# Two-layer diffusion backbone: the MLP's second product in seven block products a pair of tiles instead of eight

## The chip, the cores and the metric

The kernel runs on one core of one Trainium2 chip. The metric is the device time of one execution in microseconds. The core has TensorE (matmul, "PE"; its loads of the stationary operand are "PEld"), VectorE ("DVE"), ScalarE ("ACT"), GpSimd ("POOL") and the queue of SyncE ("SP"), which issues transfers. Matmuls write into PSUM, eight banks of 128x512 float32 values; everything else lies in SBUF, 128 partitions wide.

## What is computed

Two layers over 1024 latent and 256 context tokens, width 1024, all in float32. Each layer mixes the tokens (long convolution, retention, attention), projects, and adds an MLP with a hidden width of 4096. The change is in the MLP alone:

```python
def squared_relu_mlp(h, w1, w2):
    return jnp.square(jax.nn.relu(h @ w1)) @ w2

x = x + ga1 * (jnp.concatenate([hy, ret, att], axis=-1) @ p['w_out'])
x = x + ga2 * squared_relu_mlp(modulate(x, p['norm2_g'], sh2, sc2), p['mlp_w1'], p['mlp_w2'])
if not last:
    xc = xc + cga2 * squared_relu_mlp(modulate(xc, p['norm2_g'], csh2, csc2), p['mlp_w1'], p['mlp_w2'])
```

Layer 0 runs the MLP over 10 tiles of 128 tokens (8 latent, 2 context), layer 1 over the 8 latent ones.

## The kernel before, in words

`build` (L3146) calls one phase after the other; `phase_out` (the output projection) comes ahead of `phase_mlp`, and in layer 0 the norm of layer 1 follows, in layer 1 `phase_final`. Each phase is a block in which every engine has its own list of instructions, joined by semaphores; a `Signal` counts on through the program, and `count` works out the value to wait for. The order on each engine is written out by hand.

A float32 product is made of three passes (`three_pass`, L150 to L154) over operands split in a high part, rounded by ScalarE (a Copy into float32r), and a low part, the rest, by a subtraction on VectorE or GpSimd: high by high, high by low, low by high.

`phase_mlp` goes through the hidden width in NB = 16 blocks of FB = 256 columns, two halves of FT = 2. The tokens lie in GROUPS of 4, 4 and 2 tiles (two groups in layer 1). In a block:

- SyncE loads the next block's w1 columns (two transfers, L2977) and w2 rows (two, L2980) into `w1_raw` and `w2_raw` as soon as the low parts of this block's have been made. The first block's loads are issued by `mlp_first_loads` (L2910, L2912) at the end of `phase_out`.
- TensorE runs `steps`: up product of group 0, up of group 1, down of group 0, up of group 2 (layer 0), down of groups 1 and 2. An up product of a half is 8 k-steps (KT) of three matmuls of up to 512 tokens into one of PSUM banks 0 to 3. A down product is made for each tile t and half h of the output, two halves f of the hidden block by three passes, 128x512, into one of banks 4 to 7.
- ScalarE takes each up product through Relu (L3000), Square (L3004) and the high part (L3008), and makes the high parts of w1 (L2991) and w2 (L2996).
- VectorE makes the low parts of w1 (L3022), w2 (L3028) and the hidden values (L3036), and multiplies each down product by the gate into `mlp_tmp` (L3044).
- GpSimd adds `mlp_tmp` to x (L3063).

x stays in SBUF throughout. When a tile of x is complete, ScalarE sums its squares for the next norm (`square_sum`, L164).

Of the kernel before, what the change touches and what calls it, by code (L numbers as in the profile page):

```python
# [19 lines left out]
F32 = mybir.dt.float32  # L20
# [5 lines left out]
P = 128  # L26
# [2615 lines left out]
def phase_out(kit, l):  # L2642
# [261 lines left out]

def mlp_first_loads(kit, l, sp):

    raw1, raw2 = kit.at("w1_raw", [P, 2, 4, FB], 152), kit.at("w2_raw", [P, FB // P, D], 160)
    w1_dram, w2_dram = kit.io["mlp_w1"][l].rearrange("(t p) n -> p t n", p=P), kit.io["mlp_w2"][l]
    for i in range(2):
        sp.dma_start(raw1[:, i], w1_dram[:, 4 * i:4 * i + 4, 0:FB]).then_inc(kit.sig(f"mlp_raw{i}", 16).sem, 16)  # L2910
    for f in range(FB // P):
        sp.dma_start(raw2[:, f], w2_dram[f * P:(f + 1) * P, :]).then_inc(kit.sig(f"mlp_raw{2 + f}", 16).sem, 16)  # L2912


def mlp_gate_loads(kit, l, sp):

    gate = kit.at("gate2", [P, 2, D], 196)
    for cond in range(2):
        sp.dma_start(gate[:, cond, :], kit.gate_dram[l, 1, cond].partition_broadcast(P)).then_inc(kit.sig("mlp_gate_in", 16).sem, 16)


def phase_mlp(kit, l):

# [9 lines left out]
    w2h, w2l = hl(kit, "w2", [P, FT, D], 136)  # L2933
    raw1, raw2 = kit.at("w1_raw", [P, 2, 4, FB], 152), kit.at("w2_raw", [P, FT, D], 160)
    hh, hlo = hl(kit, "hidden", [P, 2, FT, 512], 168)
    relu, square, tmp = (kit.at(n, [P, 2, 512], 184 + 4 * i) for i, n in enumerate(("relu", "square", "mlp_tmp")))
    gate = kit.at("gate2", [P, 2, D], 196)
    steps = [("up", 0), ("up", 1), ("down", 0)] + ([("up", 2)] if n_groups == 3 else []) + [("down", g) for g in range(1, n_groups)]
# [9 lines left out]
    w1_hi, w1_lo, w2_hi, w2_lo, up, relued, squared, h_hi, h_lo, down, gated, added = sems = [kit.sig(n) for n in names]
    growth = [2, 2, FT, FT, NU, NU, NU, NU, NU, ND, ND, ND]

    raised = (relued, h_lo, added, gated, up, down)
    for s in raised:
        s.total += 1
# [4 lines left out]
    g_in.plan(range(2))  # L2958

# [5 lines left out]

    with nc.Block() as block:
        @block.sync
        def _(sp):
            w1_dram = io["mlp_w1"][l].rearrange("(t p) n -> p t n", p=P)
            w2_dram = io["mlp_w2"][l]  # L2970


            with sp.Fori(1, NB) as b:
# [4 lines left out]
                for f in range(FT):  # L2978
                    sp.wait_ge(w2_lo.sem, count(w2_lo, b - 1, f + 1))
                    sp.dma_start(raw2[:, f], w2_dram[bass.ds(col + f * P, P), :]).then_inc(w_raw[2 + f].sem, 16)  # L2980

        @block.scalar
        def _(act):
            act.sem_inc(relued.sem, 1)
            with act.Fori(0, NB // UNROLL) as loop:
                for b in [(loop, v) for v in range(UNROLL)]:
                    for i in range(2):
                        act.wait_ge(w_raw[i].sem, count(w_raw[i], b, 16))
                        if i == 0:
                            act.wait_ge(up.sem, count(up, b, 0))  # L2990
# [303 lines left out]
```

## Time and profile before

| what | value |
|---|---|
| median of three runs | 3913.89 us (3913.44 to 3917.47) |
| the profiled execution, its own time | 3917.63 us |
| its span from first to last instruction | 3915.8 us |
| granted TensorE clock, mean over the span | 0.952 |
| instructions | 53160 |

The engine times of the page are sums of the instructions' durations. Matmuls overlap one another in such a sum, so their starts, in order of time, tell what one costs. A line of the page often is that of a helper: all matmuls of a three-pass product stand under L152, L153 and L154, whichever phase issued them, and are told apart by the names of their tiles. In order of time, a row that ends in "x2" holds two instructions that followed one another directly. The two levels of TensorE's clock, 1.2 and 2.4 GHz, stand as 0.5 and 1.0; a stretch with both shows a value between.

### The profile page before, as it was taken

To read this page: it belongs to the slowest core of one execution; us is meant where nothing else is said; L and a number is where in the kernel's file an instruction comes from. 1 tells how busy PE (TensorE), PEld (TensorE's weight loads), DVE (VectorE), ACT (ScalarE), POOL (GpSimd) and SP (SyncE) were. 2 spreads that over 40 slices of the span, in tenths; PEclk is the share of its full clock that TensorE was granted. 3 is DMA by queue.
4 is the path that set the end of the run, shared out by engine and by line. 5 is a ranking of instruction groups with operands and counts; after the bars stand their busy time and mean duration, and the time that the engine had idled before them with its cause. 6 is when DMAs were issued, how large, how long until landed. Compare 5 with 4: busy or idle time off the path is not lost. (4 is left out here: it accounts for less than half of the span.)

```text
span 3915.8 us, 53160 instructions
## 1 busy us (share of the span) xinstructions
PE 3633.8 (93%) x19584; PEld 3052.4 (78%) x19584; DVE 2121.0 (54%) x3713; ACT 1412.3 (36%) x2831; POOL 1400.5 (36%) x1268
## 2 busy tenths in 40 slices
PE   7979998999679899999999899989997989999997
PEld 3668997777667688888888679978886768888886
DVE  5468535666676444444444574356675645444544
ACT  3341124666513522222222411246672252222222
POOL 1122133555100055444554421436630005445554
PEclk8989987999889999999999899879998999999999
DMA  5255201001313111111101162010014311111111
GB/s 208 93 174 183 94 10 35 12 8 40 150 63 152 44 44 32 32 43 43 43 28 37 70 200 83 11 32 11 6 39 167 151 44 54 54 43 43 54 54 48
DMA packets 153895, 266.96 MB, mean 68 GB/s; under 512 B 8968, under 2 KB 122777, under 8 KB 151290
## 3 DMA queue, kind: packets, MB, share of 16 engines
q1 hardware_dynamic: 143452, 212.38, 16.3%
q0 software_dynamic: 6352, 46.01, 3.1%
q10 hardware_dynamic: 3920, 6.29, 0.5%
q8 instruction: 107, 1.75, 0.2%
q14 instruction: 64, 0.52, 0.0%
HBM read 229.10 MB, written 33.59 MB: 67 GB/s over the span
## 5 line engine op out<-in xcount | busy, mean ns | idle before, releaser
L3063 POOL TENSOR_TENSOR x<-x,mlp_tmp 128x512 f32<-128x512 f32 x576 | 785.6, 1397 | 1324.0 <-DVE mlp_tmp L3044 1319.2
L3044 DVE TENSOR_TENSOR mlp_tmp<-psum,gate 128x512 f32<-128x512 f32 x576 | 391.8, 689 | 273.1 <-POOL x L3063 194.6
L152 PE MATMUL psum<-act_hi,w_hi 128*128 128x512 f32 (+1 forms) x1280 | 472.5, 369 | 14.1 <-DVE w_lo L3022 14.1
L153 PE MATMUL psum<-act_lo,w_hi 128*128 128x512 f32 (+1 forms) x1280 | 472.2, 369 | 0.0
L154 PE MATMUL psum<-act_hi,w_lo 128*128 128x512 f32 (+1 forms) x1280 | 471.9, 369 | 0.0
L152 PE MATMUL psum<-w_hi,hidden_hi 128*128 128x512 f32 x1152 | 449.9, 391 | 0.0
L153 PE MATMUL psum<-w_lo,hidden_hi 128*128 128x512 f32 x1152 | 448.4, 389 | 0.0
L154 PE MATMUL psum<-w_hi,hidden_lo 128*128 128x512 f32 x1152 | 448.2, 389 | 0.0
L3036 DVE TENSOR_TENSOR hidden_lo<-square,hidden_hi 128x512 fp32r<-128x512 f32 x160 | 102.3, 640 | 591.8 <-ACT hidden_hi L3008 591.8
L1981 DVE TENSOR_REDUCE att_max<-psum 128x1 f32<-128x512 f32 (+2 forms) x272 | 217.3, 799 | 261.9 <-PE psum L154 261.8
L3000 ACT ACTIVATE relu<-psum 128x512 f32<-128x512 f32 x160 | 88.9, 555 | 665.9 <-PE psum L154 665.9
L152 PEld LDWEIGHTS psum<-act_hi,w_hi 128*128 128x128 f32 x1280 | 242.2, 189 | 55.5 <-DVE w_lo L3022 14.9
L153 PEld LDWEIGHTS psum<-act_lo,w_hi 128*128 128x128 f32 x1280 | 242.2, 189 | 40.8
L154 PEld LDWEIGHTS psum<-act_hi,w_lo 128*128 128x128 f32 x1280 | 242.2, 189 | 40.2
L1805 ACT ACTIVATE probs<-psum,att_max 128x512 f32<-128x512 f32 (+2 forms) x272 | 208.7, 772 | 176.6 <-DVE att_max L1985 175.9
L152 PE MATMUL psum<-w_in_hi,act_hi 128*128 128x256 f32 (+1 forms) x912 | 259.1, 284 | 0.0
L154 PE MATMUL psum<-w_in_hi,act_lo 128*128 128x256 f32 (+1 forms) x912 | 256.7, 282 | 0.0
L153 PE MATMUL psum<-w_in_lo,act_hi 128*128 128x256 f32 (+1 forms) x912 | 256.7, 281 | 0.0
L152 PEld LDWEIGHTS psum<-w_hi,hidden_hi 128*128 128x128 f32 x1152 | 216.3, 188 | 47.5 <-DVE mlp_tmp L3044 3.7
L154 PEld LDWEIGHTS psum<-w_hi,hidden_lo 128*128 128x128 f32 x1152 | 216.3, 188 | 45.2
L153 PEld LDWEIGHTS psum<-w_lo,hidden_hi 128*128 128x128 f32 x1152 | 216.4, 188 | 43.9
L2996 ACT ACTIVATE w_hi<-w_raw 128x1024 fp32r<-128x1024 f32 x64 | 64.3, 1052 | 467.1 <-PE psum L154 467.1
(385 smaller groups left out, 8242.4 us busy)
## 6 DMA issues: line engine op xcount, KB each, us to landing
w_raw<-in_mlp_w SPq DMA_DIRECT2D x128, 512.0 KB, 3.8
side_w<-in_w_ada SPq DMA_DIRECT2D x40, 1024.0 KB, 6.3
w_raw<-in_w_in SPq DMA_DIRECT2D x32, 512.0 KB, 4.8
hy_ahead<-in_hy_ahead POOLq DMA_DIRECT2D x8, 2048.0 KB, 12.5
open_tab<-in_hy_ahead POOLq DMA_DIRECT2D x8, 1024.0 KB, 13.5
spec_scratch<-open_staged SPq DMA_DIRECT2D x16, 512.0 KB, 2.7
hy_spec<-spec_scratch SPq DMA_DIRECT2D x16, 512.0 KB, 3.6
hy_back<-in_hy_back POOLq DMA_DIRECT2D x2, 4096.0 KB, 29.7
```

The lines of the kernel that those rows point to most:

```text
L152: pe.matmul(out, lhs[0], rhs[0], start=start, stop=False)
L153: pe.matmul(out, lhs[0], rhs[1], start=False, stop=False)
L154: return pe.matmul(out, lhs[1], rhs[0], start=False, stop=stop)
L1805: act.activation(pe_[:, n % 2, at:end], psf[:, at:end], ACT.Exp, scale=SCALE, bias=mx[:, n % 2, 1:2], accum_out=sums[:, k, n % SUM_RING:n ...
L1981: dve_last = dve.tensor_reduce(mx[:, n % 2, 6 + k:7 + k], psf[:, at:at + len(part) * P], AX.X, ALU.max)
L2996: act.activation(w2h[:, f], raw2[:, f], ACT.Copy).then_inc(w2_hi.sem, 1)
L3000: act.activation(relu[:, i % 2, 0:n], ps[:, i % 4, 0:n], ACT.Relu).then_inc(relued.sem, 1)
L3036: dve.tensor_tensor(hlo[:, g % 2, f, 0:n], square[:, i % 2, 0:n], hh[:, g % 2, f, 0:n].bitcast(F32), ALU.subtract).then_inc(h_lo.sem, 1)
L3044: dve.tensor_tensor(tmp[:, j % 2, :], ps[:, 4 + j % 4, :], gate[:, int(t >= LAT_TILES), 512 * h:512 * h + 512], ALU.mult).then_inc(gated.s ...
L3063: pool.tensor_tensor(a, a, tmp[:, j % 2, :], ALU.add).then_inc(added.sem, 1)
```

## The change

The hidden block (256 tokens of a pair of tiles by 256 hidden columns) and the block of w2 (256 rows by 1024 columns) are each taken as two by two blocks. The product of two such is made of seven block products of sums of the blocks, where there were eight of the blocks themselves. `STEPS` names for each of the seven the slot of hidden sums and the slot of weight sums.

- **TensorE**: `product` makes one block product of three 128x128 by 128x512 matmuls into one bank of 4 to 7; there are 7 a pair (35 a block in layer 0, 28 in layer 1). The up product of group 0 of the next block is made during the last down group: from its fourth k-step on, each k-step is followed by one (layer 0) or two (layer 1) block products until they are all issued.
- **Weights**: SyncE loads w2's rows straight into slots 0 to 3 of `w2_sums`, and waits for all products of the block before. VectorE makes three more slots (and overwrites one) in four dependent subtractions, 128x512 each; ScalarE makes the high parts of slots 0 to 2 and 3 to 6, VectorE the low parts, in the place of the sums.
- **Hidden values**: ScalarE squares straight into slots of `hid_sums`; VectorE makes four dependent sums of 128x128 a pair; then one high part (ScalarE) and one low part (VectorE) of 128x896.
- **Adding up**: ScalarE copies the first product of a pair out of PSUM; VectorE makes seven additions out of PSUM (`add_up`), into x or into two scratch tiles; GpSimd makes four additions of scratch tiles to x (`add_shared`).
- **w1's low parts** are made by GpSimd, but for the first block's.
- **Gate and residual**: `phase_out` stores x to a scratch tensor in DRAM and no longer loads the gate. In the MLP x is set to zero by VectorE and collects the bare product. At the end SyncE loads the gate and the old x (once the last up product has been made), and `gated_tile` makes x * gate + old x, two instructions of 128x1024 a tile, on GpSimd for tiles 0 to 2 and on VectorE for the others. The squares for the norm come behind.
- Some semaphores are given back between phases (`kit.retire`).

The core of the diff:

```diff
@@ phase_out, SyncE
-            sp.wait_ge(c_lo.sem, c_lo[(3, 1)])
-            mlp_gate_loads(kit, l, sp)
-            sp.wait_ge(done.sem, done[units[-1]])
-            mlp_first_loads(kit, l, sp)
+            for j, t in enumerate(range(0, n_tiles, 4)):
+                n = min(4, n_tiles - t)
+                if t + n == n_tiles:
+                    sp.wait_ge(done.sem, done[units[-1]])
+                    mlp_first_loads(kit, l, sp)
+                sp.wait_ge(added.sem, added[(t + n - 1, 1)])
+                sp.dma_start(kit.x_dram[t * P:(t + n) * P].rearrange("(t p) n -> p t n", p=P), x[:, t:t + n, :]).then_inc(x_kept.sem, 16)
@@ phase_mlp
+STEPS = [(0, 0), (5, 1), (3, 4), (4, 2), (1, 5), (2, 3), (6, 6)]
...
+    def gated_tile(eng, sem, t):
+        c = int(t >= LAT_TILES)
+        eng.tensor_tensor(x[:, t, :], x[:, t, :], gate[:, c, :], ALU.mult).then_inc(sem.sem, 1)
+        eng.wait_ge(sem.sem, sem[(t, 0)])
+        eng.wait_ge(x_in[t // 4].sem, x_in[t // 4][0])
+        eng.tensor_tensor(x[:, t, :], x[:, t, :], x_old[:, t, :], ALU.add).then_inc(sem.sem, 1)
@@ SyncE
             with sp.Fori(1, NB) as b:
                 col = sp.snap(b * FB)
...
-                for f in range(FT):
-                    sp.wait_ge(w2_lo.sem, count(w2_lo, b - 1, f + 1))
-                    sp.dma_start(raw2[:, f], w2_dram[bass.ds(col + f * P, P), :]).then_inc(w_raw[2 + f].sem, 16)
+                sp.wait_ge(down.sem, count(down, b, 0))
+                mlp_w2_rows(kit, l, sp, col)
+            sp.wait_ge(up.sem, count(up, NB, 0))
+            for cond in range(2):
+                sp.dma_start(gate[:, cond, :], kit.gate_dram[l, 1, cond].partition_broadcast(P)).then_inc(g_in.sem, 16)
+            sp.wait_ge(x_kept.sem, kept)
+            for j, t in enumerate(range(0, n_tiles, 4)):
+                n = min(4, n_tiles - t)
+                sp.dma_start(x_old[:, t:t + n, :], kit.x_dram[t * P:(t + n) * P].rearrange("(t p) n -> p t n", p=P)).then_inc(x_in[j].sem, 16)
@@ ScalarE
+            def square(b, p):
+                act.wait_ge(relued.sem, count(relued, b, 2 * (p // 2) + 2))
+                act.wait_ge(down.sem, count(down, b, M * (p - 1)))
+                cols = slice(p % 2 * 2 * P, (p % 2 + 1) * 2 * P)
+                for f in range(FT):
+                    act.activation(hs[buffer(b, p)][:, 5 * f:5 * f + 2].rearrange("p a c -> p (a c)"), relu[f][:, cols],
+                                   ACT.Square).then_inc(squared.sem, 1)
+            def high(b, p):
+                act.wait_ge(h_sum.sem, count(h_sum, b, 4 * p + 4))
+                act.activation(hh[buffer(b, p)][:], hs[buffer(b, p)][:], ACT.Copy).then_inc(h_hi.sem, 1)
+            def copy(b, p):
+                act.wait_ge(down.sem, count(down, b, M * p + 1))
+                act.wait_ge(added.sem, count(added, b, 4 * (p - 1)))
+                act.activation(p1[buffer(b, p)][:], ps[:, 4 + M * p % 4, :], ACT.Copy).then_inc(copied.sem, 1)
+            def one_block(b, following):
...
+                copy(b, 0)
+                if n_groups == 2 and following is not None:
+                    w1_high(following)
+                copy(b, 1)
+                for p in (2, 3):
+                    square(b, p)
+                    high(b, p)
+                if n_groups == 3:
+                    positive(b, 2, 0)
+                    positive(b, 2, 1)
+                copy(b, 2)
+                if n_groups == 3 and following is not None:
+                    w1_high(following)
+                copy(b, 3)
+                if n_groups == 3:
+                    square(b, 4)
+                    high(b, 4)
+                    copy(b, 4)
@@ VectorE
+            dve.wait_ge(x_kept.sem, kept)
+            dve.memset(x[:, 0:n_tiles, :], 0.0).then_inc(zeroed.sem, 1)
...
+            def hidden_sums(b, p):
+                s = hs[buffer(b, p)]
+                dve.wait_ge(squared.sem, count(squared, b, 2 * p + 2))
+                for k, (to, i, j, op) in enumerate(((2, 1, 6, ALU.add), (1, 0, 1, ALU.subtract), (3, 2, 0, ALU.subtract),
+                                                    (4, 5, 3, ALU.subtract))):
+                    if k:
+                        dve.wait_ge(h_sum.sem, count(h_sum, b, 4 * p + k))
+                    dve.tensor_tensor(s[:, to], s[:, i], s[:, j], op).then_inc(h_sum.sem, 1)
+            def add_up(b, p, between=None):
...
+                dve.wait_ge(added.sem, count(added, b, 4 * (p - 1)))
+                for k, (out, other, n, own) in enumerate(...):
+                    dve.wait_ge(down.sem, count(down, b, M * p + n + 1))
...
+                    dve.tensor_tensor(out, other, ps[:, 4 + (M * p + n) % 4, :], ALU.add).then_inc(summed.sem, 1)
+                    if k == 3 and between is not None:
+                        hidden_sums(b, between)
...
+                    weight_sums(b)
+                    weight_low(b, 0)
+                    hidden_sums(b, 0)
+                    hidden_sums(b, 1)
+                    weight_low(b, 1)
+                    hidden_low(b, 0)
+                    hidden_low(b, 1)
+                    add_up(b, 0)
+                    add_up(b, 1, 2)
+                    hidden_low(b, 2)
+                    hidden_sums(b, 3)
+                    hidden_low(b, 3)
+                    add_up(b, 2)
+                    if NP == 4:
+                        add_up(b, 3)
+                    else:
+                        add_up(b, 3, 4)
+                        hidden_low(b, 4)
+                        add_up(b, 4)
@@ GpSimd
+            def add_shared(b, p):
+                i = buffer(b, p)
+                for what, half, h, behind in ((p1[i], 0, 0, 1), (u2[i], 0, 1, 5), (u3[i], 1, 1, 6), (u3[i], 1, 0, 7)):
+                    a = x[:, 2 * p + half, 512 * h:512 * h + 512]
...
+                    pool.wait_ge(summed.sem, count(summed, b, M * p + behind))
+                    pool.tensor_tensor(a, a, what[:], ALU.add).then_inc(added.sem, 1)
+            def one_block(b, following):
+                w1_at = 0 if n_groups == 2 else 2
+                for p in pairs:
+                    if p == w1_at and following is not None:
+                        w1_low(following)
+                    add_shared(b, p)
@@ TensorE
+            def product(b, j):
+                p, n = divmod(j, M)
...
+                if n == 0:
+                    if p == 0:
+                        pe.wait_ge(w2_lo.sem, count(w2_lo, b, 2))
+                    pe.wait_ge(h_lo.sem, count(h_lo, b, p + 1))
+                i, (u, w) = buffer(b, p), STEPS[n]
+                three_pass(pe, ps[:, 4 + j % 4, :], [a[i][:, u, :] for a in (hh, hlo)],
+                           [a[:, w, :] for a in (w2h, w2l)], True, True).then_inc(down.sem, 1)
+            def one_block(b, following):
+                for g in groups[1:]:
+                    up_group(b, g)
+                    down_group(b, g - 1)
+                if following is None:
+                    down_group(b, n_groups - 1)
+                else:
+                    j, each = 2 * M * (n_groups - 1), GROUPS[n_groups - 1][1] // 2
+                    for f in range(FT):
+                        for k in range(KT):
+                            up_step(following, 0, f, k)
+                            if f * KT + k >= 3:
+                                for _ in range(min(each, ND - j)):
+                                    product(b, j)
+                                    j += 1
```

## Rows read from the trace of the kernel before

**Rows 1.** The page: busy time, share of the span and instructions.
```profile
PE 3633.8 (93%) x19584; PEld 3052.4 (78%) x19584; DVE 2121.0 (54%) x3713; ACT 1412.3 (36%) x2831; POOL 1400.5 (36%) x1268
```

**Rows 2.** Table of stretches; columns: start:end, us, busy PE, PEld, DVE, ACT, POOL, PEclk, DMA, GB/s.
```profile
1341.40:2219.20 877.80, 877.76 (x4224) 742.10 (x4224) 381.81 (x478) 228.17 (x367) 432.24 (x319) 1.00 0.12 36
2219.20:2222.90 3.70, 0.15 (x1) 0.00 (x0) 0.69 (x1) 1.86 (x4) 2.14 (x2) 0.93 0.00 0
3194.95:3894.90 699.95, 699.94 (x3072) 576.69 (x3072) 331.42 (x382) 186.68 (x267) 349.05 (x255) 1.00 0.15 45
3894.90:3898.50 3.60, 0.17 (x1) 0.00 (x0) 0.69 (x1) 1.89 (x4) 2.16 (x2) 0.98 0.00 0
```

**Rows 3.** Order of time, TensorE in an up product; columns: start us, us, engine, line.
```profile
1358.99 0.39 PE L152 MATMUL psum<-act_hi,w_hi 128*128 128x512 f32 x1
1359.22 0.39 PE L153 MATMUL psum<-act_lo,w_hi 128*128 128x512 f32 x1
1359.44 0.39 PE L154 MATMUL psum<-act_hi,w_lo 128*128 128x512 f32 x1
```

**Rows 4.** Groups by line: one of the second product's three matmul groups.
```profile
L152 PE MATMUL psum<-w_hi,hidden_hi 128*128 128x512 f32 x1152 | 449.9, 391 | 0.0
```

**Rows 5.** Single lines (ns min/median/max), one row by time, one group by line (mean).
```profile
L3044 DVE TENSOR_TENSOR mlp_tmp<-psum,gate x576: 670/691/694, 1367.9 to 3895.1; 128x512 f32<-128x512 f32 x192
...
1422.62 1.28 DVE L3044 TENSOR_TENSOR mlp_tmp<-psum,gate 128x512 f32<-128x512 f32 x2
...
L3063 POOL TENSOR_TENSOR x<-x,mlp_tmp x576: 1260/1296/2297, 1368.7 to 3895.9; 128x512 f32<-128x512 f32 x192
...
L3022 DVE TENSOR_TENSOR w_lo<-w_raw,w_hi x64: 1214/1628/2315, 1340.2 to 3842.9; 128x1024 fp32r<-128x1024 f32 x64
...
L1571 DVE TENSOR_TENSOR k_rope_tmp<-mla,rope 128x128 f32<-128x128 f32 x2 | 0.6, 283 | 0.0
...
L1233 POOL TENSOR_TENSOR w_in_lo<-w_raw,w_in_hi x32: 1569/2400/2678, 247.2 to 2450.4; 128x1024 fp32r<-128x1024 f32 x28, 128x640 fp32r<-128x640 f32 x4
...
L752 DVE TENSOR_TENSOR factor<-factor,side_gain x6: 167/168/2355, 462.8 to 2398.8; 128x8 f32<-128x8 f32 x6
```

**Rows 6.** Order of time: VectorE and GpSimd, both reading SBUF, 1448 to 1452.
```profile
1448.20 3.45 DVE L3022 TENSOR_TENSOR w_lo<-w_raw,w_hi 128x1024 fp32r<-128x1024 f32 x2
1448.36 2.20 POOL L3063 TENSOR_TENSOR x<-x,mlp_tmp 128x512 f32<-128x512 f32 x1
...
1449.33 2.31 DVE L3022 TENSOR_TENSOR w_lo<-w_raw,w_hi 128x1024 fp32r<-128x1024 f32 x1
```

**Rows 7.** The first weight loads, lines L2910 (first pair) and L2912 (second).
```profile
L2910 SPq DMA_DIRECT2D w_raw<-in_mlp_w x4: 384/446/509, 1324.6 to 3178.6; - x4
...
DMA to landing us min/median/max: 3.8/4.3/4.9
...
DMA to landing us min/median/max: 5.5/6.2/6.8
```

**Rows 8.** Groups by line, ScalarE, 1400 to 2190: the high parts.
```profile
L2996 ACT ACTIVATE w_hi<-w_raw 128x1024 fp32r<-128x1024 f32 x29 | 29.2, 1052 | 183.1 <-PE psum L154 183.1
```

**Rows 9.** Table of stretches: TensorE after a wait (columns as in rows 2).
```profile
2959.00:2963.90 4.90, 0.01 (x1) 0.02 (x1) 4.73 (x6) 0.60 (x1) 0.00 (x0) 0.85 1.04 421
2963.90:2970.00 6.10, 6.09 (x29) 6.10 (x30) 0.00 (x0) 0.00 (x0) 0.00 (x0) 0.51 1.04 426
```

**Rows 10.** Groups by line: a memset; the page's DMA issues (KB each, us to landing).
```profile
L1456 DVE MEMSET ret_state<- 64x256 f32 x2 | 0.5, 272 | 0.0
...
gate<-gate_scratch SPq DMA_DIRECT2D x8, 512.0 KB, 11.7
x<-x_scratch SPq DMA_DIRECT2D x2, 2048.0 KB, 18.9
```

More of the change, by code:

```diff
@@ L2932, in phase_mlp @@
     w1h, w1l = hl(kit, "w1", [P, KT, FB], 120)
[L2933 to L2938, printed above, removed]
@@ L2948, in phase_mlp @@
[L2948 to L2951 removed]
+    w2h, w2l, w2s = kit.at("w2x_hi", [P, 7, 512], 136, F32R), kit.at("w2x_lo", [P, 7, 512], 160, F32R), kit.at("w2_sums", [P, 7, 512], 160)
+    raw1 = kit.at("w1_raw", [P, 2, 4, FB], 152)
+    hs = [kit.at("hid_sums", [P, 7, P], 174 + 3.5 * i) for i in range(2)]
@@ new lines, in phase_mlp @@
+    pairs = range(n_tiles // 2)
+    NP, M = len(pairs), len(STEPS)
+    NU, ND = len(ups), NP * M
+    w_raw = [kit.sig(f"mlp_raw{i}", 16) for i in range(4)]
+    g_in, norm_squared, x_kept, zeroed = kit.sig("mlp_gate_in", 16), kit.sig("nt_squared"), kit.sig("mlp_x_out", 16), kit.sig("nt_meaned")
+    x_in = [kit.sig(f"out_x{j}", 16) for j in range(3)]
+    by_pool, by_dve = kit.sig("out_gated"), kit.sig("out_added")
+    pool_tiles, dve_tiles = range(0, 3), range(3, n_tiles)
+    square_order = [3, 4, 0, 5, 6, 1, 7] + list(range(8, n_tiles)) + [2]
@@ L2958, in phase_mlp @@
     g_in.plan(range(2))
+    for sg in x_in:
+        sg.plan(range(1))
+    by_pool.plan([(t, k) for t in pool_tiles for k in range(2)])
+    by_dve.plan([(t, k) for t in dve_tiles for k in range(2)])
     def count(s, b, k):
@@ L3049, in _ @@
+            w1_high(0)
+            with act.Fori(0, NB // UNROLL - 1) as loop:
                 for v in range(UNROLL):
@@ L3055, in _ @@
         @block.gpsimd
         def _(pool):
-            pool.sem_inc(added.sem, 1)
-            with pool.Fori(0, NB // UNROLL) as loop:
-                for b in [(loop, v) for v in range(UNROLL)]:
-                    for j, (g, t, h) in enumerate(downs):
-                        a = x[:, t, 512 * h:512 * h + 512]
-                        pool.wait_ge(gated.sem, count(gated, b, j + 1))
-                        pool.tensor_tensor(a, a, tmp[:, j % 2, :], ALU.add).then_inc(added.sem, 1)
+            pool.sem_inc(added.sem, 8)
@@ new lines, in one_block @@
+            def one_block(b, following):
[4 more added lines that the diff above has]
+                    add_shared(b, p)
+            with pool.Fori(0, NB // UNROLL - 1) as loop:
+                for v in range(UNROLL):
+                    one_block((loop, v), (loop, v + 1))
+            for b in range(NB - UNROLL, NB):
+                one_block(b, b + 1 if b + 1 < NB else None)
@@ L3100, in phase_final @@
+            up_group(0, 0)
+            with pe.Fori(0, NB // UNROLL - 1) as loop:
+                for v in range(UNROLL):
+                    one_block((loop, v), (loop, v + 1))
+            for b in range(NB - UNROLL, NB):
+                one_block(b, b + 1 if b + 1 < NB else None)
 def phase_final(kit):
```

249 lines of the change are left out of this document (144 added, 105 removed).

## The prediction

> **What bounds the kernel now.** I read the busy table first: TensorE is busy for 93% of the span, VectorE 54%, GpSimd 36% [rows 1]. Then a table of stretches: the two MLPs take 877.8 and 699.95 us, and in both TensorE's busy time is the whole stretch, at the full granted clock, 2.4 GHz [rows 2]. Sixteen blocks each: 54.9 and 43.7 us a block. After the last matmul 3.7 and 3.6 us pass before the next phase. In order of time, consecutive 128x512 matmuls start 0.227 us apart [rows 3]. So until now only the count of matmuls sets the MLP, and everything else hides in it.
>
> **What is removed.** A pair of token tiles needed 8 block products, now 7, each three matmuls: 0.68 us. There are five pairs in layer 0, four in layer 1, so 15 and 12 matmuls fewer a block, 432 in all, from three groups of 1152 [rows 4]: 432 x 0.227 = 97.9 us. Ideal blocks are then 51.5 and 41.0 us. This holds only if the new sums stay beside it.
>
> **What is added, and at what price.** A 128x512 addition out of PSUM is priced by today's product of PSUM and gate: 670 to 694 ns in all 576 cases, although GpSimd was at work beside many of them; two take 1.28 [rows 5]. Seven a pair are 4.5 us against 4.8 us of products: just hidden. A subtraction of 1024 elements from SBUF takes 1.22 us at its shortest, so 1536, 2048 and 896 elements (hidden low) about 1.76, 2.29 and 1.09; one of 128 takes 0.283 [rows 5]. The 20 hidden sums and 5 low parts of a layer 0 block, with the weight sums, bring VectorE to about 42 us of the 51. GpSimd keeps 20 additions of 1.30 and gains two 1024-wide ones of 2.4. Neither is full. What matters is order: VectorE works through a hand-written list.
>
> **The lock.** The longest durations show what happens when both engines read SBUF. A GpSimd addition starts at 1448.36, in the middle of a VectorE subtraction, and takes 2.20 instead of 1.30; the next subtraction, started at 1449.33, takes 2.31 instead of 1.22 and ends 1.08 after GpSimd does [rows 6]. They take turns, a whole instruction each. A tiny one pays as well: 128x8 elements, 168 ns in the median, took 2355 ns once, about one 1024-wide GpSimd instruction [rows 5]. So each of four dependent hidden sums can wait for one GpSimd addition: 4 x (1.14 + 0.16) = 5.2 us, less what the first finds already done, for 1.2 us alone. The row is for 128x8; no row has a 128x128 sum under GpSimd additions. By the Trainium skill, "SBUF — State Buffer", section "SBUF: two separate sides", the shared port pair is locked for a whole instruction and the loser blocks fully; that speaks against this change, and rows 6 agree.
>
> **Step 1, the turn to new weights.** w2's rows now load only when the last product of the block before is done, at T. TensorE then has six k-steps of the next up product and the 10.9 us of group 1 left: 15.0 us. Against it: the two loads are issued by T+0.9, and the first pair of four such loads landed in 3.8 to 4.9 us [rows 7], so T+5.6. Then VectorE: four sums 2.8, low part 1.76, two times four hidden sums 2.4, low part 2.29, hidden low 1.09: 10.3 us. The first product starts at T+16.0: a stall of 1.0. Bounds: 0 (landing in 3.8) and 2.9 (6.8, the second pair [rows 7]). By the Trainium skill, "VectorE: DVE Perf Modes", the section on the TRN2 errata, an SBUF instruction takes 58 cycles plus one per element; that makes this chain about 8.7 us and the stall nothing. The rows of 0.283 and 1.22 us contradict it.
>
> **Step 2, inside the block.** Times from the first product. Layer 1: products of pairs 0 and 1 end at 9.5, four k-steps at 12.3. GpSimd has w1's low parts until 7.4, then additions without a gap. VectorE's fourth addition of pair 1 ends at 9.1; the hidden sums of pair 2 take turns until 13.9, three additions until 15.7, hidden low until 16.8. So product 14 waits 4.6 us. Hidden sums and low of pair 3, with ScalarE's high part (0.95, from 1.05 per 1024 elements [rows 8]) between, then hold VectorE and the copy of pair 2's first product until 22: 1.1 more. Stall 5.7. Layer 0: the third up group (5.9 us) hides pair 2, and 1.7 is left from pair 3; but the sums of pair 4 meet GpSimd straight behind w1's low parts, from 26.1 to 30.8, and its hidden low ends at 34.3 where TensorE is ready at 29.3: 5.1. Stall 6.8. Without turns the same count gives 1.1 and 1.0; these are the low bounds. If the waiting instruction is late, its queue too is late: all additions of the next pair stand behind it.
>
> **Step 3, the clock.** After 4.9 us in which TensorE did nothing (busy 0.01), it worked 6.1 us at 0.51, thus 1.2 GHz [rows 9]. Waits of 4.6 and 5.1 us in each block should do the same. Five us at half speed lose 2.5; I take 2.0 in layer 0, where products follow at once, and 1.0 in layer 1, where a second wait hides some. Bounds 0 and 3.
>
> **Step 4, the ends.** Before the first block VectorE clears x: 272 ns for 256 elements [rows 10], so 10.9 us for 10240; with the 10.3 us chain it ends just ahead of the 23.8 us that TensorE spends on two up groups: nothing. If the cover went, it would cost up to 11, once a layer. The store of x and its reload (2 MB in 18.9 us, gate 11.7 [rows 10]) lie beside 20 us of products; the reload would be the next thing late. Behind the last product the additions end at +3.4. Then gate and residual: 14 instructions of 1024 on VectorE (layer 0; 10 in layer 1), 6 on GpSimd. In turns: six rounds of 1.12 + 2.35 = 20.8 us, then eight of 1.2 (four): 30.4 (25.6). With the squares 36.6 and 31.7, against 3.7 and 3.6: +33 and +28. If both ran side by side it would be +18 and +16, the low bounds.
>
> **The sum.** Layer 0: 51.5 + 1.0 + 6.8 + 2.0 = 61.3 for 54.9, +6.4; layer 1: 41.0 + 1.0 + 5.7 + 1.0 = 48.7 for 43.7, +5.0. Over 15 blocks 96 + 75. The last blocks, without a turn, add 5 each. Ends 61. In all +242 on the profiled execution (3917.6 by its own clock, span 3915.8), 3.7 above the median of 3913.9: about 4156.
>
> **Rivals.** *The lock hardly bites small sums.* For it: 128 elements need the port for a tenth of a microsecond, and no row has just this pair of instructions. Against it: the 2355 ns. Then stalls are 1.0 + 1.0 and 1.0 + 1.1, the clock stays, blocks 53.5 and 43.1: 16 blocks give -22 and -10, ends +34 to +61: about 3918 to 3950. Half bitten, up to 4050. *Faster: the sums are truly hidden.* The place is the hidden sums behind pair 1: if GpSimd has its additions done before VectorE comes to them, and the weight rows land by T+4.6, no wait is left and only the ends cost: -98 + 34 = -64, 3850. It decides below 1.15 us of stall a block (98 less 61, over 32). For it: GpSimd's list is only 31 us of a block. Against it: this list lies just there, directly behind the products. *The clock pays more.* It falls in both waits and slows the products that release VectorE: 2 to 3 us more a block, 4220 to 4250. That the change does something else than it says has no hold in the diff: 7 products of three matmuls stand there.
>
> **Chances.** Forecast, 4050 to 4220: 0.56. Lock light, 3918 to 4050: 0.2. Faster: 0.13. Clock: 0.11. The range takes in the first two and half of the clock's case: 3925 to 4235; the faster case and a rest stay out. A measurement of this kernel tells 0.2% (8 us) from no change; only the lower edge of the light lock is within: 0.05. Faster 0.13, slower 0.82.
>
> **What would show it.** Right: the MLPs' stretches near 979 and 780 us, TensorE idle ahead of the product matmuls until VectorE's hidden low, 128x128 sums with a median far above 0.283 and many above 1.2 us, a granted clock below 1 in the MLPs, 30 us or so between the last matmul and the next phase. Wrong: hidden sums of 0.3 us, a clock of 1.00, stretches below 860 and 690, or TensorE waiting for the weights' DMA rather than for VectorE.

## The result, and the profile after

| what | before | after |
|---|---|---|
| median | 3915.5 us (3913.44 to 3917.47, 4 runs) | 4167.14 us (4149.13 to 4175.33, 4 runs) |
| the profiled execution, span | 3915.8 us | 4173.5 us |
| granted TensorE clock, mean | 0.952 | 0.924 |
| layer 0 MLP, first to last matmul; then to the next phase | 877.9; 3.6 us | 986.4; 35.7 us |
| layer 1 MLP, the same | 700.1; 3.6 us | 788.7; 31.6 us |

Slower by a ratio of 1.0636, 95% interval 1.060 to 1.0673. The forecast was 4156, the range 3925 to 4235. The four differences of the table, 108.5 + 32.1 + 88.6 + 28.0 = 257.2 us, are all but 0.5 of the 257.7 by which the span grew; the stretches outside the MLPs and their ends differ by 1.1 us at most. (The last two lines come from the order of time, as do the same lines in the table further down.)

The page's first part and three of its groups by line (busy us, mean ns | idle before, releaser), to be held against [rows 1, 4]:

```profile
PE 3633.4 (87%) x19152; PEld 3014.9 (72%) x19152; DVE 2837.4 (68%) x4799; ACT 1565.8 (38%) x3087; POOL 1570.8 (38%) x1340
...
L152 PE MATMUL psum<-w2x_hi,hid_hi 128*128 128x512 f32 x1008 | 423.4, 420 | 199.2 <-DVE hid_lo L3152 178.4
...
L3147 DVE TENSOR_TENSOR hid_sums<-hid_sums 128x128 f32<-128x128 f32 x576 | 347.6, 608 | 14.8
...
L3060 ACT ACTIVATE hid_hi<-hid_sums 128x896 fp32r<-128x896 f32 x144 | 137.2, 954 | 460.7 <-DVE hid_sums L3147 460.7
```

432 matmuls fewer, and TensorE's busy time is the same. One of the three product groups was idle 199 us before its matmuls where the group of before had 0.0 [rows 4], nearly all until VectorE's hidden low part. That waits for ScalarE's high part, which waits for the hidden sums: 608 ns in the mean each. The table of stretches (columns as in [rows 2]):

```profile
1342.30:2329.20 986.90, 878.35 (x3984) 717.57 (x3984) 745.97 (x1058) 297.84 (x478) 501.33 (x348) 0.94 0.11 38
2329.20:2364.60 35.40, 0.00 (x0) 0.00 (x0) 30.07 (x16) 11.17 (x20) 23.09 (x9) 0.56 0.00 0
3336.50:4127.60 791.10, 697.51 (x2880) 563.62 (x2880) 627.52 (x866) 254.13 (x382) 407.93 (x285) 0.95 0.14 47
4127.60:4156.20 28.60, 0.00 (x0) 0.00 (x0) 24.39 (x10) 8.63 (x15) 21.57 (x8) 0.52 0.00 0
```

Of 986.90 us TensorE works 878.35, and the granted clock is 0.94 where it was 1.00. VectorE, at 76% of the stretch, is not full, nor is GpSimd. So it looks like order and not load; the experiments put that to the test. One block of layer 0 in order of time, on VectorE, GpSimd, ScalarE and TensorE in turn (a row that ends in x4 is four instructions in a row):

```profile
1764.01 4.35 DVE L3147 TENSOR_TENSOR hid_sums<-hid_sums 128x128 f32<-128x128 f32 x4
1768.28 1.87 DVE L3167 TENSOR_TENSOR x<-x,psum 128x512 f32<-128x512 f32 x3
1770.08 1.59 DVE L3152 TENSOR_TENSOR hid_lo<-hid_sums,hid_hi 128x896 fp32r<-128x896 f32 x1
...
1764.30 3.91 POOL L3216 TENSOR_TENSOR x<-x,mlp_u 128x512 f32<-128x512 f32 x3
...
1768.39 0.95 ACT L3060 ACTIVATE hid_hi<-hid_sums 128x896 fp32r<-128x896 f32 x1 [6.76 <-DVE hid_sums L3147]
...
1771.72 0.80 PE L152 MATMUL psum<-w2x_hi,hid_hi 128*128 128x512 f32 x1 [4.27 <-DVE hid_lo L3152]
1772.31 0.63 PE L153 MATMUL psum<-w2x_lo,hid_hi 128*128 128x512 f32 x1
```

Read from the bottom. TensorE stood for 4.27 us and then ran with starts 0.43 us apart where [rows 3] have 0.227: 1.2 GHz, the lower of its two levels. It waited for a hidden low that ended at 1771.67, behind three additions, behind four sums that took 4.35 us. Exactly beside these GpSimd made three additions of 1.3 without a pause. Four sums with three additions between them: they take turns. The same place in layer 1 shows the sums of pairs 2 and 3 one behind the other, and the first of the two waits of the forecast:

```profile
3565.29 4.82 DVE L3147 TENSOR_TENSOR hid_sums<-hid_sums 128x128 f32<-128x128 f32 x4
3570.03 1.87 DVE L3167 TENSOR_TENSOR x<-x,psum 128x512 f32<-128x512 f32 x3
3571.82 1.18 DVE L3152 TENSOR_TENSOR hid_lo<-hid_sums,hid_hi 128x896 fp32r<-128x896 f32 x1
3572.93 3.29 DVE L3147 TENSOR_TENSOR hid_sums<-hid_sums 128x128 f32<-128x128 f32 x4
...
3573.05 0.80 PE L152 MATMUL psum<-w2x_hi,hid_hi 128*128 128x512 f32 x1 [4.42 <-DVE hid_lo L3152]
```

The turn to new weights, on SyncE's queue, VectorE and TensorE. After the last product TensorE goes on at 1783.04; VectorE starts on the weights at 1789.23, TensorE on the first product at 1799.60, late by 1.44.

```profile
1783.37 0.57 SPq L2925 DMA_DIRECT2D w_sums<-in_mlp_w  x1
1784.14 0.44 SPq L2926 DMA_DIRECT2D w_sums<-in_mlp_w  x1
...
1789.23 2.87 DVE L3132 TENSOR_TENSOR w_sums<-w_sums 128x512 f32<-128x512 f32 x4 [5.31 <-DMA w_sums<-in_mlp_w]
...
1798.46 2.09 DVE L3152 TENSOR_TENSOR hid_lo<-hid_sums,hid_hi 128x896 fp32r<-128x896 f32 x2
...
1799.60 0.50 PE L152 MATMUL psum<-w2x_hi,hid_hi 128*128 128x512 f32 x1 [1.44 <-DVE hid_lo L3152]
```

And the end of layer 0, gate and residual: while GpSimd has tiles left, each instruction of either engine takes 3.2 to 3.4 us; alone VectorE takes 1.23.

```profile
2337.20 3.36 DVE L3006 TENSOR_TENSOR x<-x,gate 128x1024 f32<-128x1024 f32 x1
...
2336.28 3.20 POOL L3009 TENSOR_TENSOR x<-x,x_old 128x1024 f32<-128x1024 f32 x1
...
2353.72 1.23 DVE L3009 TENSOR_TENSOR x<-x,x_old 128x1024 f32<-128x1024 f32 x1
```

### The profile page after: what moved, and what is told of

Read it like the earlier page. It is cut to its first block and busy times, and to the rows that moved or that the text cites. A ratio compares the mean times of both kernels' runs of the same rounds, so it can differ in the third digit from the quotient of the medians.

```text
span 4173.5 us, 55995 instructions
## 1 busy us (share of the span) xinstructions
PE 3633.4 (87%) x19152; PEld 3014.9 (72%) x19152; DVE 2837.4 (68%) x4799; ACT 1565.8 (38%) x3087; POOL 1570.8 (38%) x1340
## 5 line engine op out<-in xcount | busy, mean ns | idle before, releaser
L3216 POOL TENSOR_TENSOR x<-x,mlp_u 128x512 f32<-128x512 f32 x432 | 590.3, 1395 | 199.7 <-DVE x L3167 199.7
L152 PE MATMUL psum<-w2x_hi,hid_hi 128*128 128x512 f32 x1008 | 423.4, 420 | 199.2 <-DVE hid_lo L3152 178.4
L3167 DVE TENSOR_TENSOR x<-x,psum 128x512 f32<-128x512 f32 x720 | 468.3, 683 | 160.4 <-PE psum L154 149.8
L3216 POOL TENSOR_TENSOR x<-x,mlp_p 128x512 f32<-128x512 f32 x144 | 187.2, 1300 | 667.9 <-DVE x L3167 667.9
L153 PE MATMUL psum<-w2x_lo,hid_hi 128*128 128x512 f32 x1008 | 411.4, 408 | 0.0
L154 PE MATMUL psum<-w2x_hi,hid_lo 128*128 128x512 f32 x1008 | 410.4, 407 | 0.0
L152 PEld LDWEIGHTS psum<-w2x_hi,hid_hi 128*128 128x128 f32 x1008 | 200.1, 199 | 280.3 <-DVE hid_lo L3152 144.0
L3147 DVE TENSOR_TENSOR hid_sums<-hid_sums 128x128 f32<-128x128 f32 x576 | 347.6, 608 | 14.8
L3205 POOL TENSOR_TENSOR w_lo<-w_raw,w_hi 128x1024 fp32r<-128x1024 f32 x60 | 143.4, 2411 | 526.9 <-ACT w_hi L3041 526.9
L154 PEld LDWEIGHTS psum<-w2x_hi,hid_lo 128*128 128x128 f32 x1008 | 200.2, 199 | 45.2
```

What stands on the lines that cost most here:

```text
L152: pe.matmul(out, lhs[0], rhs[0], start=start, stop=False)
L153: pe.matmul(out, lhs[0], rhs[1], start=False, stop=False)
L154: return pe.matmul(out, lhs[1], rhs[0], start=False, stop=stop)
L3147: dve.tensor_tensor(s[:, to], s[:, i], s[:, j], op).then_inc(h_sum.sem, 1)
L3167: dve.tensor_tensor(out, other, ps[:, 4 + (M * p + n) % 4, :], ALU.add).then_inc(summed.sem, 1)
L3205: pool.tensor_tensor(w1l[:, 4 * i:4 * i + 4, :], raw1[:, i], w1h[:, 4 * i:4 * i + 4, :].bitcast(F32), ALU.subtract).then_inc(w1_lo.sem, 1)
```

## The experiments

The ratio is to executions of the kernel before that were made together with the variant's (their medians lie between 3914.1 and 3918.6 us). MLP is first to last matmul, end is from there to the next phase's first instruction, both from the profiled executions, layer 0 / layer 1. The profiled execution of the change, 4175.3 us, was the slowest of its four, so differences of traces come out up to 8 us larger than those of medians.

| kernel | median us (runs) | ratio to before (95%) | MLP | end |
|---|---|---|---|---|
| the change | 4167.1 (4) | 1.0636 (1.060 to 1.0673) | 986.4 / 788.7 | 35.7 / 31.6 |
| shared additions cut short | 3956.2 (2) | 1.0106 (1.0086 to 1.0127) | 863.8 / 703.3 | 33.4 / 28.7 |
| ends on VectorE | 4153.5 (4) | 1.0606 (1.0589 to 1.0624) | 986.0 / 786.0 | 29.4 / 25.2 |
| sums on GpSimd | 4020.3 (4) | 1.0269 (1.0251 to 1.0286) | 888.4 / 735.2 | 38.7 / 33.0 |
| wait filled | 4127.5 (4) | 1.0550 (1.0532 to 1.0567) | 954.9 / 773.0 | 35.7 / 31.5 |
| products denser | 4123.3 (4) | 1.0535 (1.0517 to 1.0553) | 958.3 / 768.0 | 35.7 / 31.6 |
| new orders | 3908.4 (11) | 0.9984 (0.9974 to 0.9993) | 842.2 / 681.1 | 31.0 / 25.0 |
| new orders, new ends | 3893.7 (6) | 0.9942 (0.9930 to 0.9954) | 841.9 / 675.6 | 26.2 / 21.6 |
| and the ends' turns | 3895.1 (5) | 0.9946 (0.9933 to 0.9960) | 841.7 / 677.5 | 23.9 / 19.8 |

**Shared additions cut short.** Is it the turns with GpSimd?

```diff
-                    pool.tensor_tensor(a, a, what[:], ALU.add).then_inc(added.sem, 1)
+                    pool.tensor_tensor(a[:, 0:8], a[:, 0:8], what[:, 0:8], ALU.add).then_inc(added.sem, 1)
```

> GpSimd's shared additions (add_shared) touch 8 of their 512 columns; the other 504 are left out, nothing else differs, and every wait stays. If the turns that the hidden sums take with these additions are the cause, a block's period falls from 61.6 to about 53.3 us in layer 0 and from 49.1 to about 43 us in layer 1 (the wait for new weights of 1.4 us stays), TensorE's waits of 4.3 and 4.4 us for the hidden low part shrink to about 1, the granted clock in both MLPs is 1.00, and the whole is near 3950 us. If VectorE's own load and the order of its list are the cause, the additions are innocent: periods stay within 1 us of 61.6 and 49.1 and the whole above 4130 us.

3956.2: 211 us less, near the 3950 that the turns were to give. The tile's own durations (ns, minimum/median/maximum), first of the change, then of this variant:

```profile
L3147 DVE TENSOR_TENSOR hid_sums<-hid_sums x576: 282/293/1383, 1359.2 to 4115.4; 128x128 f32<-128x128 f32 x192
```

```profile
L3147 DVE TENSOR_TENSOR hid_sums<-hid_sums x576: 281/292/295, 1353.6 to 3895.4; 128x128 f32<-128x128 f32 x192
```

The sums themselves were not touched, and not one of 576 is above 295 ns now. The MLPs lose 122.6 and 85.4 us, and the granted clock is back at 1.00:

```profile
1336.90:2201.00 864.10, 832.46 (x3984) 694.49 (x3984) 646.44 (x1057) 301.38 (x478) 157.80 (x348) 1.00 0.13 44
```

What is left above the ideal 16 x 51.5 = 824 are, by the gaps between starts, a wait of some 1.4 us a block at the turn to new weights, which this edit leaves alone, and one of 0.9 for the high part of pair 4. The edit also takes work off GpSimd (158 us in this stretch for 501), so by itself it does not tell the turns from GpSimd's load; the variant with the sums on GpSimd does. Note the median of the first line, 293: most sums are made while GpSimd is idle. The slow minority lies where it decides, and a median hides that.

**Ends on VectorE.** All tiles' gate and residual on VectorE, none on GpSimd, the squares in the order of the tiles.

```diff
-    pool_tiles, dve_tiles = range(0, 3), range(3, n_tiles)
+    pool_tiles, dve_tiles = range(0), range(n_tiles)
```

> Gate and residual of all tiles on VectorE, none on GpSimd. If the two engines take whole turns when both read SBUF, GpSimd's six instructions cost 2.1 us of turn each where VectorE's cost 1.15: the stretch behind the last product gets shorter although one engine does it all, from 29.4 to 24 us in layer 0 and from 24.6 to 19 us in layer 1, 10 to 11 us in all (about 4156 us). If they share, or run side by side, taking GpSimd's help away lengthens it: 14 instructions become 20 (layer 0) and 10 become 16 (layer 1), 7 us more each, about 4180 us.

4153.5, 13.6 less, with intervals that overlap; what shows it is the trace, where the ends are 6.3 and 6.4 us shorter and the MLPs the same within 3. In turns, this helper costs more than it takes over.

**Sums on GpSimd.** If GpSimd makes the hidden sums of pairs 2 and up itself, between its additions, there is nobody to take turns with.

```diff
 VectorE, in add_up, behind the fourth addition
-                        hidden_sums(b, between)
+                        hidden_low(b, between)
 VectorE, its list
-                    add_up(b, 1, 2)
+                    add_up(b, 1)
                     hidden_low(b, 2)
-                    hidden_sums(b, 3)
-                    hidden_low(b, 3)
-                    add_up(b, 2)
+                    add_up(b, 2, 3)
...
 GpSimd, layer 1 (in layer 0: shared 0, sums 2 and 3, shared 1, w1's low parts, sums 4, shared 2 to 4)
+                    w1_low(following)
+                    hidden_sums(b, 2)
+                    add_shared(b, 0)
+                    hidden_sums(b, 3)
+                    add_shared(b, 1)
```

> The hidden sums of pairs 2, 3 and 4 are made by GpSimd, between its own additions, so that they never have to take turns with them; VectorE's low part of pair 3 (and 4) stands behind the fourth addition of the pair before. The number of instructions is the same. If the turns are the cause, TensorE's waits inside a block nearly go, the clock stays at 1.00, periods fall to 53 to 54 us in layer 0 and 42.5 to 43.5 us in layer 1, and the whole to 3940 to 3970 us. If the order of VectorE's list alone mattered, half of that; if the load on the engines is the cause, nothing goes, as GpSimd gets even more to do: above 4130 us.

4020.3: 147 us less, but 50 above the upper edge of what was expected. The MLPs lose 98.0 and 53.5 us although GpSimd does more than in the change (584 us of layer 0's MLP for 501), so it was not its load. The sums take no turns any more and the clock is 1.00 in layer 0 and 0.99 in layer 1; a turn is left where VectorE's hidden low meets GpSimd, up to 1.93 us for 1.09. Four sums take GpSimd 2.07 us (GpSimd, ScalarE and VectorE in layer 1):

```profile
3550.19 2.07 POOL L3222 TENSOR_TENSOR hid_sums<-hid_sums 128x128 f32<-128x128 f32 x4
...
3552.29 0.95 ACT L3060 ACTIVATE hid_hi<-hid_sums 128x896 fp32r<-128x896 f32 x1 [6.33 <-POOL hid_sums L3222]
3553.15 0.58 ACT L3065 ACTIVATE mlp_p<-psum 128x512 f32<-128x512 f32 x1
...
3553.83 0.69 DVE L3167 TENSOR_TENSOR mlp_u<-mlp_p,psum 128x512 f32<-128x512 f32 x1 [2.79 <-ACT mlp_p L3065]
```

What I had not counted is the next wait behind the one removed. ScalarE sits 6.33 us in front of the high part of pair 3, and the copy of pair 2's first product, ready long before, stands behind it; VectorE waits 2.79 us for that copy, and TensorE up to 1.5 us for the PSUM bank that it frees. Both queues are in the wrong order for a wait that now ends later.

**Wait filled.** What does the lower clock cost by itself? TensorE makes 18 matmuls that nobody reads (into bank 3, free then) ahead of the product that waits longest.

```diff
+                    if fill and p == 2 * (n_groups - 1):
+                        for _ in range(6):
+                            three_pass(pe, ps[:, 3, :], [a[:, 0, 0:P] for a in (w1h, w1l)], [a[:, 0, 0:512] for a in (xh, xl)], True, True)
```

> Ahead of the product that waits for 4.3 us (layer 0) and 4.4 us (layer 1), TensorE makes 18 matmuls of 128x512 that nobody reads, 4.1 us at full speed, into a free bank of PSUM; the wait itself stays. If the clock is granted at half speed because of this wait, it stays at 1.00 now, and periods fall by 2.5 to 3 us in layer 0 and by 1.2 to 2.3 us in layer 1 (there a second wait, of 1.1 us, comes out that the slow clock hides): 55 to 80 us in all, 4090 to 4110 us. If the clock costs nothing, since VectorE is what products wait for anyway, the time stays within 10 us of 4167; if the matmuls outlast the wait, it is longer.

4127.5, 39.6 less, against 57 to 77 for the expected 4090 to 4110. The clock's part is there: the first product behind the wait is at full speed at once,

```profile
1753.30 0.50 PE L152 MATMUL psum<-w2x_hi,hid_hi 128*128 128x512 f32 x1 [0.26 <-DVE hid_lo L3152]
1753.64 0.40 PE L153 MATMUL psum<-w2x_lo,hid_hi 128*128 128x512 f32 x1
```

and the MLPs get 31.5 and 15.7 us shorter. Fifteen of the sixteen blocks have the fill, so that is 2.1 and 1.05 a block. It is what full clock gives back, and smaller than I had expected here: VectorE's work is as late as before, and faster matmuls only reach the next wait sooner. In layer 1 two such waits, which the change does not have, come out in each block; by the starts they are 0.5 and 0.4 us (the brackets count from a matmul's modelled end):

```profile
3347.00 0.50 PE L152 MATMUL psum<-w2x_hi,hid_hi 128*128 128x512 f32 x1 [0.35 <-ACT mlp_p L3065]
...
3348.24 0.50 PE L152 MATMUL psum<-w2x_hi,hid_hi 128*128 128x512 f32 x1 [0.28 <-DVE x L3167]
```

**Products denser.** Is the turn to new weights a matter of cover? The last pairs' products end earlier.

```diff
-                    j, each = 2 * M * (n_groups - 1), GROUPS[n_groups - 1][1] // 2
+                    j, each = 2 * M * (n_groups - 1), GROUPS[n_groups - 1][1] // 2 + 1
```

> The products of the last pairs follow one another closer between the steps of the next first product (two a step for one in layer 0, three for two in layer 1), so that the last of them ends 2 us (3 steps of 0.68) and 1.4 us (2 steps) earlier and the new second weights have that much more cover. Nothing is left out. The theory that the wait at the turn (1.44 us in layer 0, 1.38 in layer 1) is what the chain of new weights is late by: it goes, about 1.4 us a block in both layers, 32 blocks, some 4120 us in all, with the waits before products 14 and 28 as they are. Rival, VectorE has no time to give there: the products wait for VectorE's additions of the pair before (a wait for a PSUM bank inside the stretch takes the place of the one at the turn), and the time stays within 10 us of 4167.

4123.3, 43.8 less, where some 4120 was expected; the MLPs 28.1 and 20.7, that is 1.9 and 1.4 for each of the fifteen turns. (In layer 0 that is 0.5 more than the wait itself: the stretches at the lower clock became shorter too.) TensorE's waits (total us, times, longest), first in the change, then here, for 1400 to 2300 and 1400 to 2200 us:

```profile
PE psum L152 <- DVE hid_lo L3152: 82.6, 30, 4.4
PE psum L152 <- ACT mlp_p L3065: 18.2, 14, 1.3
```

```profile
PE psum L152 <- DVE hid_lo L3152: 56.3, 13, 4.4
```

Of the two waits for hidden low a block one is left (13 in some 13 blocks). VectorE had the time to give.

**New orders.** Nothing is computed otherwise; the lists of ScalarE, VectorE and GpSimd are rearranged with the aim that no instruction that is ready stands behind one that is not. The sums of pairs 2 and up are on GpSimd, the last pairs' products are closer together and the ends are on VectorE, as in the variants above; what each part is worth in this mixture was not taken apart. In the lists pos is Relu, sq squares, hs sums, hi and hl the high and low parts, cp the copy, a and s VectorE's and GpSimd's additions, always with the pair (and step). Layer 1:

```diff
-ScalarE: pos0.0 w2h0 pos0.1 sq.0 sq.1 w2h1 hi.0 hi.1 pos1.0 pos1.1 cp.0 w1h cp.1 sq.2 hi.2 sq.3 hi.3 cp.2 cp.3
+ScalarE: pos0.0 pos0.1 sq.0 w2h0 sq.1 w2h1 hi.0 hi.1 w1h cp.0 pos1.0 cp.1 pos1.1 sq.2 hi.2 sq.3 cp.2 hi.3 cp.3
-VectorE: ws wl0 hs.0 hs.1 wl1 hl.0 hl.1 a0.0-6 a1.0-3 hs.2 a1.4-6 hl.2 hs.3 hl.3 a2.0-6 a3.0-6
+VectorE: ws hs.0 hs.1 wl0 hl.0 wl1 hl.1 a0.0-6 a1.0-6 hl.2 a2.0-3 hl.3 a2.4-6 a3.0-6
-GpSimd: w1l s0.0-3 s1.0-3 s2.0-3 s3.0-3
+GpSimd: w1l s0.0 s0.1 hs.2 s0.2 s0.3 s1.0 hs.3 s1.1-3 s2.0-3 s3.0-3
-products a k-step of the next first product: 0 0 0 2 2 2 2 2 2 2 0 0 0 0 0 0
+products a k-step of the next first product: 0 0 0 0 3 2 2 4 3 0 0 0 0 0 0 0
```

> The same operations as the changed kernel in other orders: the hidden sums of pairs 2 and up on GpSimd between its shared additions, the copies and squares on ScalarE ahead of the work that they had been queued behind, hidden_low between additions of the pair before, the products of the last pairs packed into the middle of the next first product, and the ends on VectorE. Nothing is left out. If waits by order of queues are all that the change loses (the theory), almost no wait of TensorE is left and its clock stays up: block periods of 52.0 to 53.3 us in layer 0 and 41.8 to 43 in layer 1 against 54.9 and 43.7 before, less 25 to 43 us and less 12 to 31, plus about 43 us at the two ends: 3885 to 3925 us. Rival, the engines beside TensorE are full (VectorE and GpSimd share a port, and the seven products ask more of both): the periods stay at the 55.2 and 45.4 us that the variant with the sums on GpSimd showed, and the time is near 4007 us.

3908.4, as expected: a little faster than before, by 0.16% (0.07 to 0.26%), although the ends still cost 49 us more. Blocks of 842.2/16 = 52.6 and 42.6 us stand against 54.9 and 43.7 before. The stretches:

```profile
1341.90:2184.40 842.50, 833.15 (x3984) 695.67 (x3984) 604.86 (x865) 299.39 (x478) 596.07 (x538) 1.00 0.13 45
2184.40:2215.10 30.70, 0.00 (x0) 0.00 (x0) 24.61 (x22) 11.49 (x20) 5.14 (x5) 0.57 0.00 1
3184.80:3866.20 681.40, 665.45 (x2880) 541.78 (x2880) 518.50 (x737) 253.35 (x382) 475.33 (x411) 0.99 0.16 54
```

TensorE stands for 9 of 842.50 us. GpSimd does more than in the change, 596 us for 501: less trouble with more work, since it lies in another place.

**New ends.** The gate goes to four free PSUM banks, so that VectorE's product reads one operand there.

```diff
+            for c in range(2):
+                act.activation(ps[:, 2 * c:2 * c + 2, :].rearrange("p a b -> p (a b)"), gate[:, c, :], ACT.Copy).then_inc(gate_copied.sem, 1)
...
+        dve.wait_ge(added.sem, count(added, NB - 1, 4 * (t // 2 + 1)))
+        dve.tensor_tensor(x[:, t, :], x[:, t, :], ps[:, 2 * c:2 * c + 2, :].rearrange("p a b -> p (a b)"), ALU.mult).then_inc(by_dve.sem, 1)
```

> The orders of the variant before it, and another end: ScalarE copies the gate to four free PSUM banks beside the last products; VectorE multiplies a tile as soon as its own pair is done (it does not wait for GpSimd's last additions, a wait of 4.3 us in layer 0 and 2.9 in layer 1) and takes the gate from PSUM; the residual of every second tile is added by GpSimd. Nothing is left out. If VectorE with one operand in PSUM does not shut GpSimd out (the theory, from VectorE's 0.69 us and GpSimd's 1.25 to 1.3 side by side in the products), a pair of tiles takes VectorE three turns of 1.22, 3.7 us for 4.8: the ends get 6 + 4.3 us shorter in layer 0 and 5 + 2.9 in layer 1, 3888 to 3893 us. Rival, the two engines still take turns on every tile as they did at the end of the changed kernel (3.3 us a turn): about 7 us a pair of tiles, the ends get 4 to 8 us longer in all, 3912 to 3918.

3893.7, 14.6 less and just above the expected 3888 to 3893: faster than before by 0.58% (0.46 to 0.70%). By the trace the ends gave 4.8 and 3.3 us of it, half of what I had said. 5.5 are in layer 1's MLP, 3.2 of them in its last block, where the longest wait is 2.6 us instead of 3.7 (the variant below has 3.7 again), and 3.5 lie ahead of the first MLP. I can't show that these are gains of this edit. Why the ends gave half (VectorE, then GpSimd):

```profile
2195.64 2.34 DVE L3034 TENSOR_TENSOR x<-x,psum 128x1024 f32<-128x1024 f32 x2
2198.01 2.34 DVE L3039 TENSOR_TENSOR x<-x,x_old 128x1024 f32<-128x1024 f32 x1
...
2196.92 2.34 POOL L3039 TENSOR_TENSOR x<-x,x_old 128x1024 f32<-128x1024 f32 x1 [2.30 <-DVE x L3034]
```

Two products out of PSUM take 2.34 together with GpSimd at work; the residual, both operands in SBUF, waits for GpSimd's end at 2199.26 and ends 1.1 us behind it.

**The ends' turns.** GpSimd's residual lies beside the next pair's products instead, and the last pair is VectorE's alone.

```diff
             for t in pool_tiles:
+                pool.wait_ge(by_dve.sem, by_dve[(t + 1, 1)])
                 plus_old(pool, by_pool, t)
```

> The variant before it, with GpSimd's residual of a tile started only after VectorE's own residual addition of the pair, so that it lies beside VectorE's two gate products from PSUM of the next pair; the last pair is VectorE's alone. Nothing is left out. The trace of the variant before shows a gate product from PSUM at 1.17 us with GpSimd's addition at 2.34 beside it, and VectorE's residual addition, both operands in SBUF, stretched from 1.22 to 2.2 to 3.3 us where GpSimd's is under way. If that is the two of them excluding each other only when VectorE reads both operands from SBUF (the theory), every VectorE operation takes 1.2 us here: a pair 3.5 us for 4.6, the last one 4.7, the ends shorter by some 5 us in layer 0 and 3.5 in layer 1: 3883 to 3888 us. Rival, the stretch comes with any work of the two engines beside each other: nothing gained, 3891 to 3897 us.

```profile
2194.81 2.34 DVE L3036 TENSOR_TENSOR x<-x,psum 128x1024 f32<-128x1024 f32 x2
2197.19 1.22 DVE L3041 TENSOR_TENSOR x<-x,x_old 128x1024 f32<-128x1024 f32 x1
...
2194.97 2.36 POOL L3041 TENSOR_TENSOR x<-x,x_old 128x1024 f32<-128x1024 f32 x1 [1.16 <-DVE x L3041]
```

In the trace it is as the theory has it, 3.5 us a pair of tiles, except for the first pair or two, which still lie beside the last shared additions. But VectorE's part is only 3.2 us shorter in layer 0, not 5, and ScalarE's squares of the last two tiles, now behind each other, take 0.9 of it back: the ends are 2.3 and 1.8 us shorter. The medians, 3895.1 and 3893.7, can't be told apart. The mechanism held in the rows, and the expected 3883 to 3888 did not: 7 us too low at the least. The time lies in the range of the rival, 3891 to 3897, which only the rows rule out.

## Why the prediction was right

**What bounds, and the 98 us removed.** Right. 432 matmuls are gone, and the new orders show that a good part of their time can be had: 2.3 and 1.2 us a block below before (the ideal is 3.4 and 2.7).

**Step 1, the turn to new weights.** The mechanism was right, the size small: 1.44 us (layer 0) and 1.38 (layer 1) for 1.0. Counted from 1783.04, VectorE starts on the weights at +6.2 where I had +5.6 (issue and landing are 0.6 longer), and its chain takes 10.4 us for 10.3 (the 8.7 that stood beside it is too short). The denser products show the same step from the other side, 1.9 and 1.4 a turn. The same 0.4 us too little stands in both layers: this term of the sum was mis-sized, within its bounds of 0 and 2.9.

**Step 2, inside the block.** Layer 0: 1.7 + 5.1 said, 1.3 + 4.3 in the rows (the first is the copy behind a high part: 18.2 us in 14 waits for ScalarE's `mlp_p`). Layer 1: 4.6 + 1.1 said, 4.42 seen and the second gone, since matmuls at the lower clock arrive late enough: with the wait filled it came out, as 0.5 and 0.4. So this term was 1.2 to 1.3 too large in each. It is the step with the most in it, and two variants show its cause: short additions took 208 us off the two MLPs, and the sums on GpSimd 151.5 with GpSimd busier than in the change.

**Step 3, the clock.** 2.0 and 1.0 said; the filled wait gives back 2.1 and 1.05. That is less than the lower clock takes, see the next sum: part of its loss hides waits that come out without it.

**What the blocks add up to.** They came out at 61.6 and 49.3 us for 61.3 and 48.7. Take for each matmul the distance to the next start less 0.227, in thirteen blocks from the middle of each MLP of the change. Layer 0: 51.5 of matmuls, three waits of 4.5, 1.5 and 1.4 (7.3 together), and 2.9 in matmuls that start more than 0.25 us apart, nearly all at the lower clock: 61.7. Layer 1: 40.9, two waits of 4.6 and 1.5, and 2.2 of the clock: 49.1. Nothing is left over. By this count (from starts, not from modelled ends) the turn was 1.4 and 1.5 for 1.0, the block's inside 5.9 and 4.6 for 6.8 and 5.7, the clock 2.9 and 2.2 for 2.0 and 1.0. One term was too large and two too small; that the forecast came within 11 us of 4167 is in part the luck that they cancel.

**Step 4, the ends.** +33 and +28 said, +32.1 and +28.0 measured. Turns of 3.3 us, then 1.2.

**The rivals.** "The lock hardly bites small sums" falls: 4.35 us for four, and 293 ns as soon as GpSimd's additions are short. Yet one sign that I had named, a median far above 283, was wrong: it is 293. Only 7 of a layer 0 block's 20 sums, and 6 of layer 1's 16, are stretched. The other sign, many above 1.2 us, is there: 172 of 576. (That rival's 3918 to 3950 should have been 3916 to 3943 by its own terms.) "The clock pays more" falls: the lower clock follows one wait a block and not both, and takes 0.9 and 1.2 us more than the forecast had, not 2 to 3. "Faster: the sums are truly hidden" names the right place: with the sums out of the turns, new orders and shorter ends it did come out faster. Its price, 3850, was too good: in the variant with the lowest median the ends cost 26.2 + 21.6 - 7.2 = 40.6 us, not 34, and its blocks of 52.6 and 42.2 us stand 1.1 and 1.2 above the ideal.

## What to carry over

Where two engines exclude each other, the price of a small instruction is that of the other engine's large one, and a chain of four dependent ones pays it four times. Ask of every instruction on a chain what the neighbour does at that moment, and look at its longest durations, not at the median. When a wait is taken out, follow each queue to what stands behind the next late instruction: here the move of the sums was worth 147 us, and the reordering of the three lists, with the last products closer together and the ends on VectorE, another 112. And a helper that takes twice as long for the same work made a region of turns longer; give it work at moments when the other engine does not need what it locks.

## What the runs showed of the hardware

- VectorE with one operand in PSUM is not held up by GpSimd: 1.17 us for 128x1024 (two in 2.34) with GpSimd's 2.34 to 2.36 beside it, unstretched on both sides; with both operands in SBUF 1.22 became 1.8 to 3.4 where GpSimd was under way. By the Trainium skill, "SBUF — State Buffer", section "SBUF: two separate sides", the lock concerns a VectorE instruction with two SBUF inputs against a GpSimd one that reads SBUF; the rows agree.
- GpSimd makes a 128x128 sum in 0.46 us (0.52 in a dependent row of four, 2.07) where VectorE alone needs 0.29; in turns most of VectorE's took 1.2 to 1.4, and a chain of four up to 4.8. The slower engine was the better place here.
- By the starts, the waits of 4.4 to 4.8 us in the change were each followed by 2.6 to 5.5 us of matmuls 0.43 us apart, 1.2 GHz. In layer 0 of the variant with the sums on GpSimd no wait was above 1.8 us, and the clock stayed at 2.4 GHz. The length of a wait alone does not tell: in the last block of layer 0 a wait of 2.0 us with the new orders was followed by 3.0 us at 1.2 GHz, one of 3.7 us with the short additions by none.
